# Other SBUF addresses for the second block's weight halves and activation planes

## The reference

```python
h = modulate(rmsnorm(x, norm1_g), sh1, sc1)
q, k, v, f, hy = split_projection(h @ w_in)
kc, vc = split(modulate(rmsnorm(ctx, norm1_g), csh1, csc1) @ w_in[:, 1024:3072])
a = neighbourhood_attention(q, k, v, kc, vc, na_rpb)
y = merge_groups(a, fourier_mix(f), hyena_mix(hy, ...), mix_norm_g)
x = x + g1 * (y @ w_out)
gate, up = split(modulate(rmsnorm(x, norm2_g), sh2, sc2) @ ffn_w_up)
x = x + g2 * ((gelu(dwconv(gate)) * up) @ ffn_w_down)
return rmsnorm(x, final_norm_g)
```

## Time and profile before

| | |
|---|---|
| median of 3 runs | 2189.77 us (2189.66 to 2190.39) |
| the profiled execution, its own time | 2188.41 us |
| its span, first to last instruction | 2186.6 us |
| PE busy | 2153.6 us, 98% |
| PEld busy | 2011.2 us, 92% |
| DVE busy | 1466.1 us, 67% |
| ACT busy | 1038.0 us, 47% |
| granted TensorE clock | 0.998 of full speed |

### The profile page before, as it was taken

The page is one execution under the profiler, slowest core; times in us unless marked ns, Lnnn a source line. Parts: engine busy times, 40 slices in busy tenths (PEclk is TensorE's granted clock), DMA queues, the critical chain, the costliest instruction groups (busy, mean ns, idle before and its releaser), DMA issues.

```text
span 2186.6 us, 38030 instructions
## 1 busy us (share of the span) xinstructions
PE 2153.6 (98%) x16496; PEld 2011.2 (92%) x16496; DVE 1466.1 (67%) x1850; ACT 1038.0 (47%) x1418; POOL 25.0 (1%) x47
## 2 busy tenths in 40 slices
PE   7999999999999999999999999999999999999998
PEld 7989989989999999998888999999999999998886
DVE  7666546767766797696665677788666665555665
ACT  6554434444454555454433454565444443444454
POOL 0000000110000000000000000000000000000000
PEclk9999999999999999999999999999999999999999
DMA  9765655775458878786565656766676775555553
GB/s 324 241 205 192 194 193 175 239 235 174 138 170 271 292 234 279 259 282 218 175 205 192 217 169 210 244 214 230 231 248 220 239 234 187 185 192 193 193 193 115
DMA packets 339156, 470.05 MB, mean 215 GB/s; under 512 B 14797, under 2 KB 312557, under 8 KB 326126
## 3 DMA queue, kind: packets, MB, share of 16 engines
q1 hardware_dynamic: 337838, 466.93, 64.3%
q0 software_dynamic: 1152, 0.70, 0.1%
HBM read 464.80 MB, written 2.10 MB: 214 GB/s over the span
## 4 chain that ended last, share of the span: by engine, by line
PE 95%; DVE 2%; ACT 1%; issue 0%; DMA 0%; SPq 0%; ACTq 0%; DVEq 0%
PE ps L1961 69%; PE ps L1972 10%; PE ps L1980 4%; PE ps L1992 1%; PE ps L2050 1%; DVE wlo L1181 1%; PE ps L2311 1%; PE ps L2251 1%; PE ps L2245 1%; PE ps L2213 1%; ACT whi L585 1%; PE ps L1916 0%; PE ps L2110 0%; PE ps L2205 0%; PE ps L2131 0%
## 5 line engine op out<-in xcount | busy, mean ns | idle before, releaser
L1181 DVE TENSOR_TENSOR wlo<-raw,whi 128x1024 fp32r<-128x1024 f32 (+1 forms) x668 | 815.0, 1221 | 675.5 <-ACT whi L585 673.5
L585 ACT ACTIVATE whi<-raw 128x1024 fp32r<-128x1024 f32 (+1 forms) x668 | 706.1, 1058 | 1087.9 <-PE ps L1961 887.5
L1961 PE MATMUL ps<-phi,whi 128*128 128x256 f32 (+1 forms) x3552 | 729.5, 286 | 0.9 <-DVE plo L1825 0.9
L1961 PE MATMUL ps<-plo,whi 128*128 128x256 f32 (+1 forms) x3552 | 705.9, 280 | 0.0
L1961 PE MATMUL ps<-phi,wlo 128*128 128x256 f32 (+1 forms) x3552 | 705.3, 280 | 0.0
L1961 PEld LDWEIGHTS ps<-phi,whi 128*128 128x128 f32 x3552 | 542.4, 188 | 34.0 <-issue 29.9
L1961 PEld LDWEIGHTS ps<-phi,wlo 128*128 128x128 f32 x3552 | 541.4, 188 | 0.5
L1961 PEld LDWEIGHTS ps<-plo,whi 128*128 128x128 f32 x3552 | 541.3, 188 | 0.5
L1247 DVE SCALAR_TENSOR_TENSOR arena<-raw,cst,arena 128x1024 f32<-128x1024 f32 x120 | 153.5, 1279 | 2.8
L1972 PE MATMUL ps<-whi,dhi 128*128 128x512 f32 x336 | 89.8, 389 | 0.0
L1972 PE MATMUL ps<-whi,dlo 128*128 128x512 f32 x336 | 89.8, 389 | 0.0
(11 more groups left out here) (374 smaller groups left out, 2364.2 us busy)
## 6 DMA issues: line engine op xcount, KB each, us to landing
raw<-w_in_dram SPq DMA_DIRECT2D x151, 1024.0 KB, 5.9
raw<-ada_w_dram SPq DMA_DIRECT2D x96, 1024.0 KB, 5.0
raw<-ffn_w_up_dram SPq DMA_DIRECT2D x88, 1024.0 KB, 5.1
raw<-ffn_w_down_dram SPq DMA_DIRECT2D x44, 1024.0 KB, 5.1
raw<-w_out_dram SPq DMA_DIRECT2D x32, 1024.0 KB, 5.7
raw<-w_branch_dram SPq DMA_DIRECT2D x16, 1024.0 KB, 6.1
arena<-xT_dram SPq DMA_DIRECT2D x4, 544.0 KB, 6.6
arena<-ctxT_dram SPq DMA_DIRECT2D x1, 2048.0 KB, 9.5
```

Of the source, the lines that this page charges most:

```text
L585: nc.scalar.activation(whi[c % 4][:, 0:w], src, ACT.Copy).then_inc(S("split_hi"), 1)
L1181: v.tensor_tensor(wlo[c % 4][:, 0:w], src, whi[c % 4][:, 0:w].bitcast(F32), ALU.subtract).then_inc(S("split_lo"), 1)
L1961: l = mm(ps[2 * p + h][0:m, b:b + tt.stop - tt.start], wx[:, k], x[:, xi, tt], start=first, stop=last)
```

## The change

Three things change, all of them addresses, and one wait.

1. From phase E on (`START["E"]`, chunk 196) the weight halves go to eight other buffers, `whi[4..7]` and `wlo[4..7]`, which lie 16 floats (64 bytes) above the first eight and overlap them. Modulo 256 they start at 192.
2. The planes that F, IH, IF, J, IQ, OB and L (after its sixth unit) read move from `phi`, `plo` to `f_hi`, `f_lo`, in the same memory (`phi` is not read after GB). Their rows are 256 floats, without a gap, and start at 64 modulo 256: 128 bytes from the weights. `y_lo` moves by 48 floats, from 192 to 128 modulo 256, as `y_hi`. The planes `y_hi`, `c_hi`, `c_lo`, `o_hi`, `o_lo`, `e_hi`, `e_lo`, `dhi`, `dlo` stay.
3. Since a new buffer overlaps two old ones, `hi(c)` waits for one chunk more in three places: at c = 196, 197 and 198 for `mm` at c - 2.

In bytes from the start of the weights' slice to the start of the plane's row, modulo 256, the phases go: F, IH, IF, J, IQ, OB, L from 0, 64, 128, 192 in turn (64 kt) to 128 throughout; E from 0 (high) and 64 (low) to 192; G, H, OA, M0, M1 from 0 to 192; the first six units of L from 32 kt to 32 kt + 192.

```diff
@@ -194,14 +194,23 @@
         wlo = [sb(f"wlo{i}", [128, CW], F32R) for i in range(4)]
+        whi += [at(f"whi{4 + i}", [128, CW], MEM + RING * RW + CW * i + 16, F32R) for i in range(4)]
+        wlo += [at(f"wlo{4 + i}", [128, CW], MEM + RING * RW + CW * (4 + i) + 16, F32R) for i in range(4)]
+        def slot_of(c):
+            return c % 4 + (4 if c >= START["E"] else 0)
         phi = sb("phi", [128, KT, T], F32R)
...
         r_lo = at("r_lo", [128, KT, T], base + 22928, F32R)
+        f_hi = at("f_hi", [128, KT, 256], base - 8704 + 48, F32R)
+        f_lo = at("f_lo", [128, KT, 256], base - 4352 + 48, F32R)
         y_hi = at("y_hi", [128, KT, 256], base + 12288, F32R)
-        y_lo = at("y_lo", [128, KT, 256], base + 23696, F32R)
+        y_lo = at("y_lo", [128, KT, 256], base + 23744, F32R)
         c_hi = at("c_hi", [128, KT, 256], base + 4096, F32R)
@@ -581,8 +590,9 @@
                 if c >= 4:
-                    act.wait_ge(S("mm"), c - 3)
-                nc.scalar.activation(whi[c % 4][:, 0:w], src, ACT.Copy).then_inc(S("split_hi"), 1)
+                    act.wait_ge(S("mm"), c - 2 if START["E"] <= c < START["E"] + 3 else c - 3)
+                nc.scalar.activation(whi[slot_of(c)][:, 0:w], src, ACT.Copy).then_inc(S("split_hi"), 1)
@@ -984,7 +994,7 @@
                 act.wait_ge(S("res_tmp"), 16 * k + kt + 1)
-                nc.scalar.activation(phi[:, kt, 0:256], ptmp[:, kt % 2, 0:256], ACT.Identity, bias=shift).then_inc(S("res_hi"), 1)
+                nc.scalar.activation(f_hi[:, kt, :], ptmp[:, kt % 2, 0:256], ACT.Identity, bias=shift).then_inc(S("res_hi"), 1)
@@ -1045,7 +1055,7 @@
                 if 0 <= g < 4:
-                    pair_hi(4 + g, 2 * g, phi[:, 2 * g:2 * g + 2, 0:256], 4 + g % 2)
+                    pair_hi(4 + g, 2 * g, f_hi[:, 2 * g:2 * g + 2, :], 4 + g % 2)
@@ -1097,7 +1107,7 @@
                     act.wait_ge(S("merged"), i)
-                    nc.scalar.activation(phi[:, 2 * i - 2:2 * i, 0:256], rx(gates[:, 0, 512 * i - 512:512 * i], 2), ACT.Copy)\
+                    nc.scalar.activation(f_hi[:, 2 * i - 2:2 * i, :], rx(gates[:, 0, 512 * i - 512:512 * i], 2), ACT.Copy)\
                         .then_inc(S("y_hi_set"), 1)
@@ -1178,7 +1188,7 @@
                 dve.wait_ge(S("split_hi"), c + 1)
-                v.tensor_tensor(wlo[c % 4][:, 0:w], src, whi[c % 4][:, 0:w].bitcast(F32), ALU.subtract).then_inc(S("split_lo"), 1)
+                v.tensor_tensor(wlo[slot_of(c)][:, 0:w], src, whi[slot_of(c)][:, 0:w].bitcast(F32), ALU.subtract).then_inc(S("split_lo"), 1)
@@ -1686,7 +1696,7 @@
                 dve.wait_ge(S("res_hi"), 16 * k + kt + 1)
-                v.scalar_tensor_tensor(plo[:, kt, 0:256], ptmp[:, kt % 2, 0:256], shift, phi[:, kt, 0:256].bitcast(F32), ALU.add, ALU.subtract)\
+                v.scalar_tensor_tensor(f_lo[:, kt, :], ptmp[:, kt % 2, 0:256], shift, f_hi[:, kt, :].bitcast(F32), ALU.add, ALU.subtract)\
                     .then_inc(S("res_lo"), 1)
@@ -1787,7 +1797,7 @@
                 if 0 <= g < 4:
-                    pair_lo(4 + g, plo[:, 2 * g:2 * g + 2, 0:256], phi[:, 2 * g:2 * g + 2, 0:256])
+                    pair_lo(4 + g, f_lo[:, 2 * g:2 * g + 2, :], f_hi[:, 2 * g:2 * g + 2, :])
@@ -1822,8 +1832,8 @@
                     dve.wait_ge(S("y_hi_set"), 4 + i)
-                    v.tensor_tensor(plo[:, 2 * i - 2:2 * i, 0:256], rx(gates[:, 0, 512 * i - 512:512 * i], 2),
-                                    phi[:, 2 * i - 2:2 * i, 0:256].bitcast(F32), ALU.subtract).then_inc(S("y_lo_set"), 1)
+                    v.tensor_tensor(f_lo[:, 2 * i - 2:2 * i, :], rx(gates[:, 0, 512 * i - 512:512 * i], 2),
+                                    f_hi[:, 2 * i - 2:2 * i, :].bitcast(F32), ALU.subtract).then_inc(S("y_lo_set"), 1)
                 context(c)
@@ -1910,7 +1920,7 @@
                 kd = 4 * (len(UNITS) % 2 ^ 1) + q
-                w = (CHUNKS - 4 + q) % 4
+                w = slot_of(CHUNKS - 4 + q)
                 for x, wx, last in ((dhi, whi[w], False), (dlo, whi[w], False), (dhi, wlo[w], q == 3)):
@@ -1929,8 +1939,8 @@
                     pe.wait_ge(S(f"gemm_free{p}"), (u - p) // 2)
-                wh, wl = whi[c % 4], wlo[c % 4]
-                xh, xl = {"E": (y_hi, y_lo), "G": (c_hi, c_lo), "H": (c_hi, c_lo)}.get(name, (phi, plo))
+                wh, wl = whi[slot_of(c)], wlo[slot_of(c)]
+                xh, xl = {"E": (y_hi, y_lo), "G": (c_hi, c_lo), "H": (c_hi, c_lo)}.get(name, (phi, plo) if kind in ("Tall", "Tx", "K") else (f_hi, f_lo))
                 if name == "FB":
```

## The result

The change takes 2197.48 us (median of 6 runs, 2196.17 to 2203.38) against 2189.72 us before (2188.12 to 2190.44): ratio 1.0043, 95% interval 1.003 to 1.0056. It is slower by 7.8 us; the forecast was 16.2 us faster. The profiled execution took 2196.17 us, its span is 2194.3 us, 7.7 more than before, with a granted clock of 0.997 against 0.998.

A forecast was written before the change was run, and what follows sets the result against it. TensorE was taken as the bound, busy 98% of the span, its step set by addresses. Terms -4.5 - 2.7 - 2.7 - 0.8 - 2.1 - 5.4 + 2 = -16.2 us gave a median of 2173.6 us, whole range 2150 to 2189.

The forecast's parts named there:

- That addresses set the step: In TensorE's matmuls, the distance of streaming and loading addresses within 256 bytes sets the step, 113 to 120 ns.
- The term of most planes: F, IH, IF, IQ, OB, most of L, and J: 6720 matmuls at distance 128, 116.2 ns instead of 117.0, -5.4 us.
- the stall: At chunk 204 in E, the later wait delays a load and TensorE comes earlier: 0.5 to 3.3 us, taken as +2.
- Both readings that narrowed x: For the step at distance 128 in most planes: halfway between 118 and 113 gives 115.5 ns, the round's sum gives 117.
- a fall along the round: In most planes, the penalty falls evenly from distance 64 to 192, putting the step at 128 halfway, 115.5 ns.
- 128 is bad: Rival, chance 0.16: most planes' step at distance 128 is 120 ns, 2199.2 us in all; it decides from 118.6 ns.
- the likeliest case: The forecast, chance 0.5: step at distance 128 in most planes between 115 and 118 ns, 2173.6 us, range 2165 to 2186.
- M0 and M1: Phases with 512 columns, going from distance 0 to 64: 2 ns by 1056 matmuls, -2.1 us, bounds nothing and -7.4.
- E, G, H, OA: Phases with new distances and shorter steps: E -4.5 us, G -2.7, OA -2.7, H -0.8.
- The supply rival: Chunk 204 waits its full 3.3 us and DVE sums delay TensorE as much again: 2176 to 2177 us, within the forecast's 0.5.

The follow-up runs named there:

- m1_field: A kernel of TensorE alone, 44 series of matmuls differing only in streaming and loading addresses: 120.0 ns a step at distance 0, 118.4 at 128, 113.2 at 64.
- e2_planes: Kernel before with only the planes moved, to 64 (distance 192); weights at 128, no later wait, y_lo as before: 2171.44 us, ratio 0.992.
- e3_weights: The change, but plane rows are 1088 bytes again, keeping the round of four distances against weights at 192: 2189.77 us, ratio 0.9999.
- e5_f128: The change with f_hi and f_lo another 64 bytes up, at 128, so distance 192 against weights at 192: 2173.75 us, ratio 0.9922.
- e1_wait: Kernel before with only the later wait, hi of chunks 196 to 198 one chunk later: 2191.97 us against 2189.78, ratio 1.0013.
- e7_fixed: e5_f128 with weights at 192 from the start of the kernel and no later wait: 2169.66 us, ratio 0.99 to the kernel before.
- e8_fixed_m: e7_fixed with dhi and dlo 16 floats further, so M0 and M1 are at distance 0 again: 2168.74 us, ratio 0.9896 to the kernel before.
- e6_three: The change with weights at 192 from GB, 128 again from L, planes and M at distances 192 and 0, later waits at GB and L: 2178.07 us, ratio 0.9942.

## Why the prediction was wrong

**That addresses set the step: right.** m1_field has it without the kernel, and e2_planes, e3_weights and e5_f128 turn it on and off. The rule of the Trainium skill that spoke against it ("TensorE: Matmul & The Clock Gate", Step-by-step: what each phase is for, two independent read ports) does not hold here: equal matmuls take 113.3 or 120.0 ns as their two addresses lie (m1_field, lines 28 and 30). What the Trainium skill says in "SBUF — State Buffer", Who interferes with whom, that TensorE never waits on anyone, gives no warning of this: in m1_field nothing but TensorE runs in those series, and its own two streams by their addresses set the step. How they disturb each other is not shown.

**The term of most planes: this failed, and takes the whole gain.** I put x, the step at distance 128, at 116.2 ns; it is 118.65. By my own terms that is 6720 by +1.65 = +11.1 us instead of -5.4, and the phases show +10.5 (J and parts of IH and IQ were above 117 before). The forecast of -16.2 becomes -0.3 by that alone; M and the stall make it a loss. Both readings that narrowed x took steps inside the round of four for steady ones. Six matmuls after another distance do not show it: 128 has 117 in the round and 118.65 by itself, 64 has 118 in the round and 113.3 or 117.8 by itself, so 118 at 64 was not the steady step that I called it. And "a fall along the round" assumed that the step is smooth between 64 and 192, where the field is rough. The rival "128 is bad" had this mechanism, named its point of decision (118.6) and got 0.16. That its 2199.2 us for x = 120 lies near the median, 2197.5, is luck: with x = 118.65 its sum gives 2190.1 us, and the rest is M and the stall. What the rows before supported was only the bounds, 113 to 120, and they left more on that side than I gave it. (The range of the likeliest case was summed wrongly too: x = 115 with no stall gives 2163.6 us, not 2165.)

**M0 and M1: the wrong sign.** -2.1 us was predicted with bounds of 0 and -7.4; it is +2.3 (step 226.7 to 228.9 ns). I carried the order of the steps over from 256 columns to 512. At 512 columns distance 0 is the best of the eight measured, and every other distance costs 2 to 8 ns. The lower bound of nothing was not one: no row gave a reason that a loss was excluded.

**The stall: right in place and cause, too small.** PE's wait is 2.65 us, inside 0.5 to 3.3, with ACT waiting for the load before it. SP's queue shows the chain as predicted:

```profile
719.63 0.37 SPq L413 DMA_DIRECT2D raw<-w_branch_dram  x1
...
726.16 0.92 SPq L413 DMA_DIRECT2D raw<-w_branch_dram  x1
```

The branch load is issued at 719.63 instead of 716.46, the load for chunk 204 at 726.16 instead of 723.41. Missing from the term is what comes after an idle TensorE, in the windows behind it:

```profile
744.50:746.00 1.50, 1.50 (x9) 1.50 (x10) 1.33 (x2) 1.50 (x3) 0.00 (x0) 0.67 0.96 371
746.00:748.00 2.00, 2.00 (x11) 2.00 (x11) 1.93 (x3) 1.48 (x2) 0.00 (x0) 0.50 1.10 352
748.00:750.00 2.00, 2.00 (x18) 2.00 (x17) 2.00 (x2) 0.00 (x0) 0.00 (x0) 0.89 1.10 347
```

The granted clock goes from 1.00 (2.4 GHz) to 0.50 (1.2 GHz) for some 3.4 us in all, a pair takes 0.43 us (746.36 to 746.79) instead of 0.23, and chunk 204 lasts from 744.48 to 748.94, 4.46 us instead of 2.7. With 2.8 us of lateness that is 4.6 us, against +2 in the sum. The idle times of 2.68 us in e3_weights and 3.13 in e5_f128 at this place were followed by half clock too; e1_wait, with 1.64 us, kept its clock here.

**E, G, H, OA: about right in sum, not one by one.** E's step gained 4.3 us (-4.5 predicted). H gained 2.6 us (-0.8): at distance 64 it ran at 113.3, not 118. G gained 1.8 and OA 1.3 (-2.7 each), since some of their chunks ran at 117.8. I took 113 at distance 192 for one value; it has two.

**The supply rival** is refuted as a cause: outside chunk 204 no wait grew by more than some tenths (F's wait for `f_lo` from 0.88 to 1.24 us). It has a part in e7_fixed and e8_fixed_m, where that wait is some 2.5 us.

Together: 15.9 us from the planes (-5.4 to +10.5), 4.4 from M, 2.6 from the stall, 0.7 from E, G, H and OA, 0.4 in the first block, less 0.1 in L's first six units: 23.9 us, the way from -16.2 to +7.7.

What stays open: why the step has this shape over the distance, what in the work before picks the state of 64 and 192 (the one distance before does not settle it), by what F ran in different states in two executions, and when an idle time of about 2 us is followed by half clock. e5_f128, e7_fixed and e8_fixed_m have J and most of IQ at 117.8; if they could be held at 113.3, some 5 us more are there (1152 matmuls by 4.5 ns).

## What to carry to other kernels

Where TensorE is the bound and every matmul has its own weight load, measure the step over the distance between the streaming and the loaded address in a small kernel of TensorE alone, with the column count that the kernel uses, before moving any buffer: the best and the poorest place were 6% apart, and one number per plane made 23.7 us of 2197. Don't read a steady step off a few matmuls between others, and don't bound an unmeasured step by nothing on the side that you would rather not have. Give buffers their final place from the start of the kernel: moving them halfway needed a later wait, which made a stall wherever it was put, at E's start and, as far as the coincidence in e6_three tells, in the attention before GB.

## What the runs showed of the hardware that was not expected

- The step of 256-column matmuls goes from 113.3 to 120.0 ns with the distance between streaming and loaded addresses modulo 256, at 0 and 128 whatever the roles, the weights' place or another 16 or 32 KB. It changes over 16 bytes: distance 0 has 120.0, 16 has 113.3, 48 has 118.3.
- At distances 64 and 192 there are two steps, 113.3 and 117.8 ns. One is kept for hundreds of matmuls and can change when something else ran between; what distance ran just before does not settle which, and the same kernel had both in the same phase in two executions. Distance 32 had 116.7 and 117.8.
- With 512 columns the order is another: 226.7 ns at distance 0, 228.9 at 64, 232 to 234 at the others that were measured.
- An idle time of TensorE of 2.65 us was followed by some 3.4 us at 1.2 GHz (windows above), three of 2.1 to 2.2 us in e6_three by 13.7 us in all, and one of 1.64 us by none. One of 1.90 us at the same place of the program was followed by 3.4 us in e1_wait and by none in the kernel before.
- With 13.7 us at 1.2 GHz in it instead of 3.4, the first block took 4.2 to 4.6 us longer at the same distances (e7_fixed and e8_fixed_m against the kernel before).
